# A layered trunk with streamed float32 weights: six shared raw-and-low slots, six high slots, splitting five units ahead

## The reference

```python
for i in range(2):
    h = rms_norm(x, g_mix[i]); proj = h @ w_in[i]
    # ya: gated linear recurrence (4 heads), yb: sliding-window attention (8 heads)
    x = x + (sigmoid(gate_a) * (ya @ w_pa[i]) + sigmoid(gate_b) * (yb @ w_pb[i])) @ w_o[i]
    h2 = rms_norm(x, g_ffn[i])
    if i == 0: x = x + (silu(h2 @ wg) * (h2 @ wu)) @ wd                    # D_FF = 3584
    else:      x = x + sum_e gate[:, e] * swiglu(h2, wg[e], wu[e], wd[e])  # top 2 of 8 experts
    x = x + sigmoid(rms_norm(x, g_ple[i]) @ w_ple_gate[i]) * (p[i] @ w_ple_up[i])
```

## Time and profile before

| | us |
|---|---|
| median of 3 runs (lowest, highest) | 1728.32 (1727.18, 1732.02) |
| the profiled execution's own time | 1729.72 |
| its span, first to last instruction | 1727.9 |
| PE busy in the span | 1676.2 (97%) |
| DVE busy | 1337.8 (77%) |
| ACT busy | 1093.1 (63%) |
| POOL busy | 59.3 (3%) |
| 442 low parts (L782), mean 2.290 each | 1008.6 |
| 442 high parts (L535), mean 1.918 each | 846.0 |
| mean transfer rate over the span | 274 GB/s |

### The profile page before, as it was taken

The page is one execution under the profiler, slowest core; times in us unless marked ns, Lnnn a source line. Parts: engine busy times, 40 slices in busy tenths (PEclk is TensorE's granted clock), DMA queues, the critical chain, the costliest instruction groups (busy, mean ns, idle before and its releaser), DMA issues.

```text
span 1727.9 us, 20964 instructions
## 1 busy us (share of the span) xinstructions
PE 1676.2 (97%) x7899; PEld 1390.2 (80%) x7899; DVE 1337.8 (77%) x1097; ACT 1093.1 (63%) x902; POOL 59.3 (3%) x54
## 2 busy tenths in 40 slices
PE   7999899999999998899999999999999999999997
PEld 6888788888778887788788888888887887887886
DVE  6785645445567765788889898998998998888895
ACT  5555343443455554677777777777778778777774
POOL 0100000000001000110000000000000000000000
PEclk9999999999999999899999999999999999999999
DMA  8433555555354435599999999999999999999990
GB/s 308 163 122 122 170 172 194 183 183 194 139 189 141 141 127 159 185 367 381 344 375 372 349 377 365 349 376 352 359 387 346 359 385 348 368 367 355 369 374 26
DMA packets 199550, 472.60 MB, mean 274 GB/s; under 512 B 8592, under 2 KB 11216, under 8 KB 199504
## 3 DMA queue, kind: packets, MB, share of 16 engines
q1 hardware_dynamic: 197936, 466.20, 75.6%
q0 software_dynamic: 1568, 5.77, 0.9%
HBM read 469.84 MB, written 2.10 MB: 273 GB/s over the span
## 4 chain that ended last, share of the span: by engine, by line
PE 91%; DVE 5%; ACT 3%; issue 1%; DMA 0%; SPq 0%; DVEq 0%; ACTq 0%
PE ps L1284 28%; PE ps L1286 28%; PE ps L1285 28%; PE ps L1289 4%; DVE w_lo L782 2%; ACT w_hi L535 2%; PE ps L1612 1%; ACT hT_hi L547 0%; DVE inner_lo L788 0%; PE ps L1533 0%; PE ps L1375 0%; PE ps L1394 0%; DVE hT_lo L840 0%; DMA param_rows<-in_k_norm 0%; PE ps L1296 0%
## 5 line engine op out<-in xcount | busy, mean ns | idle before, releaser
L782 DVE TENSOR_TENSOR w_lo<-raw,w_hi 128x2048 fp32r<-128x2048 f32 x442 | 1008.6, 2290 | 268.3 <-ACT w_hi L535 265.4
L535 ACT ACTIVATE w_hi<-raw 128x2048 fp32r<-128x2048 f32 x442 | 846.0, 1918 | 382.7 <-PE ps L1286 373.8
L1284 PE MATMUL ps<-w_hi,hT_hi 128*128 128x512 f32 (+1 forms) x1600 | 632.2, 395 | 8.5 <-DVE hT_lo L840 4.6
L1286 PE MATMUL ps<-w_hi,hT_lo 128*128 128x512 f32 (+1 forms) x1600 | 622.5, 389 | 0.0
L1285 PE MATMUL ps<-w_lo,hT_hi 128*128 128x512 f32 (+1 forms) x1600 | 622.1, 389 | 0.0
L1284 PEld LDWEIGHTS ps<-w_hi,hT_hi 128*128 128x128 f32 x1600 | 302.1, 189 | 75.0 <-DVE hT_lo L840 5.3
L1286 PEld LDWEIGHTS ps<-w_hi,hT_lo 128*128 128x128 f32 x1600 | 301.8, 189 | 63.5
L1285 PEld LDWEIGHTS ps<-w_lo,hT_hi 128*128 128x128 f32 x1600 | 302.4, 189 | 58.9
L1284 PE MATMUL ps<-w_hi,inner_hi 128*128 128x512 f32 x608 | 239.8, 394 | 9.4 <-DVE inner_lo L788 9.4
L1286 PE MATMUL ps<-w_hi,inner_lo 128*128 128x512 f32 x608 | 238.4, 392 | 0.0
L1285 PE MATMUL ps<-w_lo,inner_hi 128*128 128x512 f32 x608 | 238.3, 392 | 0.0
(11 more groups left out here) (229 smaller groups left out, 787.9 us busy)
## 6 DMA issues: line engine op xcount, KB each, us to landing
raw<-in_w_moe_gate SPq DMA_DIRECT2D x112, 1024.0 KB, 6.6
raw<-in_w_moe_up SPq DMA_DIRECT2D x112, 1024.0 KB, 6.9
raw<-in_w_moe_down SPq DMA_DIRECT2D x112, 1024.0 KB, 6.6
raw<-in_w_in SPq DMA_DIRECT2D x38, 1024.0 KB, 5.5
raw<-in_w_dense_gate SPq DMA_DIRECT2D x14, 1024.0 KB, 5.0
raw<-in_w_dense_up SPq DMA_DIRECT2D x14, 1024.0 KB, 5.1
raw<-in_w_dense_down SPq DMA_DIRECT2D x14, 1024.0 KB, 4.9
raw<-in_w_o SPq DMA_DIRECT2D x8, 1024.0 KB, 5.0
```

The lines of the kernel that those rows point to most:

```text
L535: nc.scalar.activation(w_hi[:, n % SLOTS, :], raw[:, n % RAW_SLOTS, :], ACT.Copy).then_inc(high_ready, 1)
L782: nc.vector.tensor_tensor(w_lo[:, n % SLOTS, :], raw[:, n % RAW_SLOTS, :], w_hi[:, n % SLOTS, :].bitcast(F32), ALU.subtract).then_inc(low_ ...
L1284: nc.tensor.matmul(o, x_parts[0][x_cols], parts[0], start=first, stop=False)
L1286: return nc.tensor.matmul(o, x_parts[1][x_cols], parts[0], start=False, stop=last)
```

## The change

`w_lo` gets the addresses of `raw`: the low part of a unit is written over its raw values. `w_hi` has six slots. A load now waits until the unit six back has been used by TensorE, and ScalarE waits for the same unit before it writes the high slot. `keep_up` splits until `used + LEAD` units are split, with LEAD = 5. The units prefetched behind the last item are five instead of four.

```diff
-SLOTS = 3
+SLOTS = 6
+LEAD = 5
...
-    END = MOE + GATE_UNITS
+    END = MOE + LEAD
...
+        RAW_AT = (nc.sbuf_base + 31) // 32 * 32
         raw = sb("raw", [P, RAW_SLOTS, UNIT])
+        w_lo = nc.alloc_sbuf_tensor_at("w_lo", [P, RAW_SLOTS, UNIT], F32R, offset=RAW_AT)
         w_hi = sb("w_hi", [P, SLOTS, UNIT], F32R)
-        w_lo = sb("w_lo", [P, SLOTS, UNIT], F32R)
...
                 if n >= RAW_SLOTS:
-                    sp.wait_ge(low_ready, n - RAW_SLOTS + 1 + items * PER_ITEM)
+                    sp.wait_ge(units_used, n - RAW_SLOTS + 1 + items * PER_ITEM)
...
-            for n, source in enumerate(PLE_UNITS[1][:GATE_UNITS]):
+            for n, source in enumerate(PLE_UNITS[1][:LEAD]):
                 load_unit(MOE + n, source, count)
...
-                while split[0] < (used + SLOTS if end is None else min(used + SLOTS, end)):
+                while split[0] < (used + LEAD if end is None else min(used + LEAD, end)):
...
-            keep_up(MIX0 + 1 - SLOTS)
+            keep_up(MIX0 + 1 - LEAD)
...
-                    nc.vector.tensor_tensor(w_lo[:, n % SLOTS, :], raw[:, n % RAW_SLOTS, :],
+                    nc.vector.tensor_tensor(w_lo[:, n % RAW_SLOTS, :], raw[:, n % RAW_SLOTS, :],
...
-                parts = [a[:, n % SLOTS, :].rearrange("p (k n) -> p k n", n=width)[:, k, cols] for a in (w_hi, w_lo)]
+                parts = [a[:, n % slots, :].rearrange("p (k n) -> p k n", n=width)[:, k, cols]
+                         for a, slots in ((w_hi, SLOTS), (w_lo, RAW_SLOTS))]
```

## The result

The changed kernel takes 1868.16 us (median of 4 runs, 1854.17 to 1869.18) against 1730.17 for the kernel before on the same occasion (4 runs): a ratio of 1.078, with a 95% interval of 1.073 to 1.084. It is slower by 138 us; the forecast was 103 us more and a time of 1831. The profiled execution has a span of 1865.9 us and a mean granted clock of 0.982, where before it was 0.991.

The account below looks back on a forecast made before the run. TensorE was taken to bound the expert stage; stalls of 12.0 us an item over eight items (96 us), 6 for the gather and 1 at the start made 103, laid on 1728.3: 1831 us, range 1780 to 1895.

Parts of the forecast that it names:

- L: Time from SyncE's issue of a load to its landing; taken as 5.2 us in the expert stage.
- The moved release: Loads wait for TensorE's product, not lo; called the costing step: L+0.2 less the product time of one unit.
- the gather: Next tokens' gather beside a load once an item: 0 to 1.4 us, taken 0.7; 6 us in all.
- silu of step 0: Expert stage, start of an item: step 1's gate product waits for this activation, 1.35 us.
- the gated product: Step 0 of an item: VectorE must first finish lo of units 7 and 8; stall 1.65 us.
- the item's end: Last down product of an expert item waits for inner_lo behind lo of unit 43: cost 0.75 us.
- rival A: The queue stays full: expert-stage landings stay at 6.8 us; 186 us more, 1914 us; chance 0.15.
- rival D: The clock: step 0's two stalls halve the clock for 6 us an item; 24 us more, 1855 us; chance 0.07.
- Two-tile stages, start, in-place write: Dense and mixer stages: taken 0 (-3 to +3 us); kernel start: taken 1 (0 to 4.6); lo over raw: taken 0.
- Rival B: Absorption: only step 0 and the item's end pay, 30 us in all, 1758 us; chance 0.12.
- steps 2 to 6: Expert stage: TensorE stalls for inner_lo, 1.92 us in steps 5 and 6, 1.47 in steps 2, 3 and 4.
- Rival C: Not slower: landings short enough, L ≤ 3.3 us; about -13 us, 1715 us; chance 0.04.

Follow-up runs that it names:

- lead4: The changed kernel with LEAD 4 in place of 5: 1733.82 us, ratio 1.0027 against the kernel before.
- the order runs: Changed kernel, LEAD still 5, activations moved ahead of keep_up calls in four cumulative runs: ratios 1.0330, 1.0216, 1.0144, 1.0072 against the kernel before.
- LEAD 3: The changed kernel with LEAD 3 in place of 5 and four units behind the last item: 1727.24 us, ratio 0.9988 against the kernel before.

## Why the prediction was right, and where it was short

**The number.** The measured 1868 us is inside the range of 1780 to 1895 and 3 us above the narrower band, 1811 to 1865, that the forecast itself was given. Direction, place and mechanism are right; 35 us of the 138 were not in the sum.

**What bounds the kernel, and the mechanism.** Right. TensorE's rate bound the expert stage, and the change put L+hi+lo ahead of the activations. `lead4` shows that it is the one step by which an issue is late, and the order runs show that it is the order: the waits for landings stayed, the stalls went.

**The moved release is what costs.** Only in company. Alone it costs 0.1%; with a lead of five it costs 138 us. The prediction's formula (through at T(u-1)+0.2+L+hi+lo) already said so, its heading did not.

**The terms**, each as idle time in the timeline of TensorE in the item from 1148.5 plus 0.16 us, beside the forecast: steps 2 and 4 1.38 and 1.56 (1.47), step 5 1.91 and step 6 1.67 (1.92), step 3 3.06 (1.47, plus 0.7 for the gather), silu of step 0 1.87 (1.35), the gated product 1.37 (1.65), the item's end 1.95, less 1.14 before, 0.8 (0.75); sum 13.6 and, by the item's length, 14.2 against 12.7. L was 5.1 in the median from 900 to 1700 us, with 5.2 forecast:

```profile
DMA to landing us min/median/max: 4.7/5.1/7.3
```

Two small sums of the prediction don't come out of its terms: the last low part of an item ends 9.66 us after T(38), not 9.9, which makes that term 0.5, and L of 5.0 gives 1821, not 1811, as the lower end of its band.

**The gather** is the term that was sized wrong: 0.7 us an item, 6 in all, of a bound of 1.4, 11 in all. It took 1.6 us of waiting even in the items where it took least, above the bound, and 20.2 in all, with 5.1 of clock behind that.

**Slow landings in runs** were left out of the sum. In the first and the last item landings stayed between 7 and 8 us for a step or more (here from 745 to 757 us), and the waits were 3.7 and 4.1 us:

```profile
DMA to landing us min/median/max: 7.5/7.7/7.9
```

The first item took 143 us, 5 more than the others. The run without the gather tells most of these apart. In the changed kernel 32 loads of the expert stage took over 6.5 us to land, without the gather 6, all issued from 743 to 758 us, ahead of the first item's gather. So the queue that does not drain by itself, rival A, was right for one step of one item, and its cause there is open; the rest is the gather.

**The clock** was rival D with a chance of 0.07, and its 24 us were not in the sum. It fell at nine places of the expert stage, 15.4 us in all. Its place was wrong: not the two stalls of step 0, but seven times the longer waits, of 2.8 to 4.1 us, six of them in step 3. One of these, the window behind the wait of 3.44 us that ended at 1338.7:

```profile
1340.00:1344.00 4.00, 4.00 (x12) 3.14 (x11) 4.00 (x4) 3.01 (x2) 0.00 (x0) 0.57 0.07 26
```

The length of the last wait doesn't decide it: it fell after the waits of 2.85 and 3.44 us, not after those of 2.90, 2.99 and 3.31, and twice after one of 1.8 or 1.9. Without the gather, five of its six falls followed waits of 1.8 to 1.9. What else decides is open. The clock is also most of the spread of the runs: spans of 1852.3 and 1867.3 us had clocks of 0.985 and 0.977, which is 28 and 43 us below full. The profiled execution is the exception, for its clock of 0.982 explains 6 of the 14 us that it lies above the fastest.

**Two-tile stages, start, in-place write.** Right within 4 us: the expert stage began 4.5 us later than before, with 1 forecast. F's transposes at the start waited 2.0 us (1 taken, 4.6 the bound); low parts took 2.289 us in place and 2.290 apart.

**The sum.** The 134.7 us of the expert stage are 107.3 more idle time in 65 waits in place of 9, 9 hidden in matmul ends, 15.4 of clock, and 3 not placed. The forecast had 102 for the same: short by 15 of clock, 14 for the gather's waits, and about 3 that hold the first item's slow landings.

**Rival B** (absorption) fell: five waits of steps 2 to 6 are in every item. Only step 1 was free of one, as worked out. **Rival C** fell with no landing below 4.6 us.

**The rules.** The page "DMA: Bandwidth & Descriptors" of the Trainium skill, section "Specifications", puts HBM near 358 GB/s for one core. This case disagrees for a core that runs alone: 406 GB/s over 3 us, 397 over 4 us with LEAD 3 (1088 to 1092 us), and a LEAD 3 item ran at 365 over 122 us. The page "HBM Reference" of the Trainium skill, section "Specifications (TRN2)", says that a core that streams alone gets well above its share. The short stretches agree; 365 is barely above it. The prediction's other reading, landings of 4.4 us and a total of about 60, fell too: none of the 443 loads landed in under 4.6 us.

## What to carry to other kernels

A deeper prefetch on an engine that also carries activations is a wait put ahead of them: before deepening it, follow one call to the last thing that it waits for, and count from that thing's issue to the consumer, landing included. With a shared slot (raw and low in one) the look-ahead must be at least two units shorter than the number of slots here, for a landing (5.1 us) takes two products (2.7 us each). Or the activations are put ahead of the wait, which gave back most of the loss as well. And a single stall of 3.6 us in a dense stretch of matmuls is to be priced with the lower clock behind it, 1.5 us a time in these runs (12.3 us over eight).

## What the runs showed of the hardware

Long landings in a profile (6.8 us at a DMA share of 1.00) can be an effect of early requests alone: with requests put off, the same bytes in the same time landed in 5.2 us, and the share stayed at 1.00. An indirect gather of half a unit's bytes lengthened the landings of the loads beside it from 5.1 to 6.7 us, and to 7.9 in the last item. The granted clock fell to the lower of its two levels, 1.2 of 2.4 GHz, for 3.4 us at each of eight single waits of 3.64 us, though TensorE was busy for the 120 us ahead of it. In other runs here it also fell after waits of 1.8 us and stayed up after one of 3.57.
